# Output projection of a hybrid decoder block's second tokens in column passes, and its first expert block gathered in fp32

## The chip, the cores and the metric

The kernel runs on one core of one Trainium2 chip. The metric is device microseconds of one execution, the median of several. Every time below is in microseconds (us) unless marked ns.

## The reference

256 tokens of 1024 channels get 16 meta tokens ahead of them and pass one decoder layer: a state-space branch and a convolution branch, merged by gates, and then a mixture of 32 experts of which every token takes 4. What the change touches is the end of the first part and the experts:

```python
h = h + _hybrid_mixer(_rmsnorm(h, norm_mix_g), ...)      # ends in: merged @ w_out
h = h + _moe(_rmsnorm(h, norm_ffn_g), ...)
out = _rmsnorm(h, norm_final_g)[:, 16:]

def _rmsnorm(x, g):  return x * rsqrt(mean(x * x) + 1e-6) * g
def _moe(hf, ...):
    top_val, top_idx = lax.top_k(hf @ router_w + router_b, 4);  probs = softmax(top_val)
    for e in range(32):
        gu = hf @ w_gate_up[e] + b_gate_up[e];  g, lin = gu[:, :1024], gu[:, 1024:]
        g = min(g, 7);  lin = clip(lin, -7, 7)
        out += combine[:, e] * ((g * sigmoid(1.702 * g) * (lin + 1)) @ w_down[e] + b_down[e])
```

Everything is float32. The weights of one expert are 8.4 MB (gate and up) and 4.2 MB (down); all 32 experts' are read, 402.7 MB.

## The kernel before, in words

The tokens stand in two groups of 128, written c = 0 and c = 1. Each engine has its own program, and semaphores join them. `wait_ge` halts an engine's queue until a count is reached, and `link` makes an engine wait for its own last instruction.

**Up to the router.** TensorE (PE) computes the mixer in a fixed order. The output projection `merged @ w_out` is a loop over c, over eight slices k of 128 inputs and over two halves h of 512 outputs, in PSUM banks 4 + 2c + h (L1415 to 1433). Within c = 1, after k = 1, PE transposes the first tokens' residual (`residual_cols(0)`, L1401) and after k = 3 it multiplies them by the router (`logits(0)`, L1410); both follow for c = 1 after the loop. VectorE (DVE) has `second_norm(c)`: add the projection to the residual h2 (L1038), copy half of the transposed residual out of PSUM (L1041), the mean square (L1044), 1/sqrt by five linked operations (L761 to 765), and the normed tokens hf = h2 * scale * norm_ffn_g with the columns rearranged (L1050). ScalarE (ACT) copies the other half (L698), sums the squares (L701) and takes the root (L703). `choose(c)` (L1059 to 1074) is the top-4 choice: twelve small operations on 128x32 that end in `masks`. `weigh(c)` is the softmax of the four. DVE's order is second_norm(0), choose(0), weigh(0), second_norm(1), choose(1).

**Three bf16 parts.** A gather of tokens for an expert is a matmul with a one-hot matrix. So that it is exact in bf16, hf is split into three bf16 parts `hp`: ACT casts (L706, L709), GpSimd (POOL) subtracts (L572, L576), once for each c and half. `parts` counts what is done.

**Plan.** After both masks PE counts the tokens of each expert (L1542 to 1546), after it has put h2 into PSUM as the sum to which experts add (`residual`, L1442, eight matmul records ahead of the counting in PE's order). DVE makes positions and the first one-hot (L1104 to 1106, L1091), PE puts the bias (L1496) and gathers block 0 (L1450, 48 matmuls), ACT copies the gathered tokens to `xT` (L717), and PE begins with expert 0. The rest of the plan (which block is which expert, to `plan`) is computed between the first blocks' matmuls.

**Expert blocks.** A block is up to 64 tokens of one expert; here there are 35 blocks, so three experts have two. In `one_block` PE runs gate and up (L1476, eight slices k, of which two are one DMA piece of 2 MB), then `middle` (scatter of the block before, L1459; gather of the next, L1450; transposes, L1509 and L1514), then down (L1487, two DMA pieces of 2 MB). DVE clamps and multiplies, ACT has the sigmoid (L723) and the copies `actT` (L725), `xT` (L727) and `ysb` (L729).

**Weights.** SyncE (SP) issues the loads in a fixed order. Each waits until the buffer's last user on PE is done (`gu_done`, `dn_done`, L451 and L457); there are buffers for two experts, in `ring`, and the odd experts' first two pieces in `late` and `early`, over hf and h2. Expert 1's pieces 0 and 1 are issued after `parts` and after the counting matmuls.

**End.** After the last block ACT loads the Sqrt table (L739), squares both groups (L742) and DVE and ACT scale and store.

## Time and profile before

| what | value |
|---|---|
| runs | 1199.01 us median of 3 (1197.71 to 1199.34) |
| the profiled execution | 1199.63 us, its span from first to last instruction 1197.6 us |
| granted TensorE clock | 0.995 of full speed |
| busy share | PE 94%, DVE 27%, ACT 16%, POOL 4% |
| DMA | 436.43 MB, mean 364 GB/s, 428 to 430 GB/s in most slices of the second part |
| the first expert block begins | 237.05 us from the span's start |
| the last down projection begins | 1177.32 us |

The profiled execution's own time is 2.0 us over its span; the span is what views of the trace divide up. In a row of the timeline stand start, duration, engine, line of the kernel, operation, output <- inputs, shapes and count, and in brackets how long the engine had been idle and who released it. One float32 matmul with 128 columns of weights is two records, in `x16` too.

### The profile page before, as it was taken

The numbers are of one execution on the slowest core, as the hardware profiler recorded it, in microseconds if no ns is written. First come the engines' busy times: TensorE is split into PE (matmuls) and PEld (weight loads), VectorE is DVE, ScalarE is ACT, GpSimd is POOL, SyncE is SP. The second block draws the span as 40 slices with busy tenths as digits, with TensorE's granted clock in tenths as the row PEclk, the third lists the DMA queues.
The fourth block names the chain that finished last, engine by engine and source line by source line (L and its number), as shares of the span: only waits on it lengthen the run. The fifth ranks groups of instructions, "written<-read, shape, count | busy, mean of one in ns | idle before, by whom it ended". The sixth has DMA issues, their size and how long they took to land.

```text
span 1197.6 us, 17762 instructions
## 1 busy us (share of the span) xinstructions
PE 1127.9 (94%) x7148; PEld 532.1 (44%) x7149; DVE 324.9 (27%) x765; ACT 188.1 (16%) x279; POOL 43.8 (4%) x45
## 2 busy tenths in 40 slices
PE   8999999899999999989999998888888999999995
PEld 6887886443334333333343333333333334333332
DVE  5999462631122111111121111111111112111112
ACT  2311230411111111111111111111111111111002
POOL 1102230300000000000000000000000000000000
PEclk9999999999999999999999999999999999999998
DMA  9672593692999999997999999999999799999994
GB/s 263 216 203 94 202 386 123 242 408 100 430 429 428 429 428 428 429 428 310 414 429 428 428 428 429 429 428 429 429 429 428 334 387 429 429 427 428 428 428 177
DMA packets 57399, 436.43 MB, mean 364 GB/s; under 512 B 11056, under 2 KB 27504, under 8 KB 32704
## 3 DMA queue, kind: packets, MB, share of 16 engines
q1 hardware_dynamic: 57232, 436.02, 88.3%
q8 instruction: 16, 0.26, 0.1%
q10 hardware_dynamic: 144, 0.09, 0.0%
q14 instruction: 7, 0.06, 0.0%
HBM read 432.72 MB, written 1.05 MB: 362 GB/s over the span
## 4 chain that ended last, share of the span: by engine, by line
PE 70%; DMA 25%; ACT 2%; issue 1%; DVE 1%; ACTq 0%; SPq 0%; DVEq 0%
PE ps L1476 30%; DMA ring<-in_w_gate_up 25%; PE ps L1487 14%; PE ps L1238 8%; PE ps L1459 4%; PE ps L1450 2%; PE ps L1378 2%; PE ps L1425 2%; PE ps L1324 1%; PE ps L1509 1%; PE ps L1390 1%; ACT rD L725 1%; PE ps L1496 1%; PE ps L1289 0%; PE ps L1203 0%
## 5 line engine op out<-in xcount | busy, mean ns | idle before, releaser
L1476 PE MATMUL ps<-ring,rD 128*64 128x512 f32 x1664 | 368.1, 594 | 32.0 <-DMA ring<-in_w_gate_up 31.7
L1487 PE MATMUL ps<-ring,rD 128*64 128x512 f32 x1120 | 248.0, 595 | 16.0 <-ACT rD L725 15.9
L1476 PEld LDWEIGHTS ps<-ring,rD 128*64 128x64 f32 x1664 | 119.8, 137 | 266.0 <-issue 209.9
L1487 PEld LDWEIGHTS ps<-ring,rD 128*64 128x64 f32 x1120 | 79.8, 137 | 157.6 <-issue 157.3
L1160 DVE TENSOR_SCALAR rD<-ps 128x512 f32<-128x512 f32 x35 | 24.2, 691 | 424.3 <-PE ps L1476 424.3
L723 ACT ACTIVATE rD<-rD 128x512 f32<-128x512 f32 x35 | 22.0, 630 | 493.7 <-DVE rD L1160 493.7
L1238 PE MATMUL ps<-ring 128*128 128x256 f32 (+1 forms) x384 | 87.4, 386 | 0.0
L1086 DVE CAST rE<-rE 128x64 bf16 (+1 forms) x36 | 7.0, 195 | 294.4 <-PE ps L1476 294.1
L1238 PEld LDWEIGHTS ps<-ring 128*128 128x128 f32 x384 | 72.1, 190 | 12.7 <-issue 1.4
L1459 PE MATMUL ps<-rD,rE 64*128 64x512 f32 x288 | 71.6, 615 | 0.7 <-ACT rD L729 0.7
L1450 PEld LDWEIGHTS ps<-rE,rC 128*128 128x128 bf16 x1728 | 58.3, 99 | 27.3 <-issue 26.9
L1476 PE MATMUL ps<-late,rD 128*64 128x512 f32 x288 | 64.9, 592 | 0.0
L1476 PE MATMUL ps<-early,rD 128*64 128x512 f32 x288 | 64.9, 592 | 0.0
L1450 PE MATMUL ps<-rE,rC 128*128 128x64 bf16 x1728 | 63.5, 195 | 0.0
L729 ACT COPY rD<-ps 128x512 f32<-128x512 f32 x35 | 20.5, 585 | 243.7 <-PE ps L1487 243.7
L1459 PEld LDWEIGHTS ps<-rD,rE 64*128 64x128 f32 x288 | 24.8, 186 | 46.9 <-issue 45.4
L723 ACT ACT_TABLE_LOAD x32 | 41.1, 1283 | 6.3 <-DVEq L1123 5.7
L1476 PEld LDWEIGHTS ps<-early,rD 128*64 128x64 f32 x288 | 21.4, 137 | 40.4 <-issue 40.4
L1476 PEld LDWEIGHTS ps<-late,rD 128*64 128x64 f32 x288 | 21.2, 136 | 33.4 <-issue 30.4
L725 ACT COPY rD<-ps 128x512 f32<-128x512 f32 x35 | 20.5, 585 | 80.4 <-PE ps L1509 80.4
L1425 PE MATMUL ps<-ring,late 128*128 128x512 f32 x64 | 28.0, 593 | 0.0
L1378 PE MATMUL ps<-late,ring 128*128 128x256 f32 x128 | 27.8, 379 | 0.0
(332 smaller groups left out, 726.3 us busy)
## 6 DMA issues: line engine op xcount, KB each, us to landing
ring<-in_w_gate_up SPq DMA_DIRECT2D x96, 2048.0 KB, 20.6
ring<-in_w_down SPq DMA_DIRECT2D x64, 2048.0 KB, 24.5
late<-in_w_gate_up SPq DMA_DIRECT2D x16, 2048.0 KB, 24.4
early<-in_w_gate_up SPq DMA_DIRECT2D x16, 2048.0 KB, 28.8
ring<-in_w_in SPq DMA_DIRECT2D x14, 1024.0 KB, 7.9
ring<-in_w_out SPq DMA_DIRECT2D x4, 1024.0 KB, 17.0
ring<-late SPq DMA_DIRECT2D x16, 142.0 KB, 2.8
ring<-in_w_s_lin SPq DMA_DIRECT2D x2, 1024.0 KB, 5.0
```

Of the source, the lines that this page charges most:

```text
L723: nc.scalar.activation(sg, g1, ACT.Sigmoid, scale=ALPHA).then_inc(sg_ready, 1)
L725: nc.scalar.copy(actT, ps[:, 0, :].rearrange("p (j s) -> p j s", s=P)).then_inc(actT_ready, 1)
L729: nc.scalar.copy(ysb, ps[:, 2, :]).then_inc(y_ready, 1)
L1160: nc.vector.tensor_scalar(g1, ps[:, 0, :], LIMIT, None, ALU.min).then_inc(g1_ready, 1)
L1238: ins = nc.tensor.matmul(ps[:, z % 2, 0:L - n0], w[:, k, (z % 2) * P:(z % 2) * P + P], h[:, k, n0:L], start=(k == 0), stop=(k == KT - 1))
L1324: ins = nc.tensor.matmul(ps[32 * g:32 * g + 32, 3, (m % 2) * S:(m % 2) * S + S], wtap[:, a, g, :], shifted[:, m, g, SH * a:SH * a + S], st ...
L1378: ins = nc.tensor.matmul(ps[:, bank(use), g * S:(g + 1) * S], w[:, k, (n % 4) * P:(n % 4) * P + P], ya[:, k, :], start=(k == 0), stop=(k = ...
L1425: ins = nc.tensor.matmul(ps[:, 4 + 2 * c + h, :], merged[:, k, c * P:(c + 1) * P], w[:, k % 2, 512 * h:512 * h + 512], start=(k == 0), sto ...
L1450: ins = nc.tensor.matmul(ps[:, 3, k * BS:(k + 1) * BS], hp[:, part, c, k * P:(k + 1) * P], onehot[:, c, :], start=(c == 0 and part == 0), ...
L1459: ins = nc.tensor.matmul(ps[:, 4 + 2 * c + h, :], selT[64 * h:64 * h + 64, c * P:(c + 1) * P], ysb[64 * h:64 * h + 64, :], start=False, st ...
L1476: ins = nc.tensor.matmul(ps[64 * h:64 * h + 64, a, :], xT[:, k, :], gsl[odd][n][:, at:at + 512], start=False, stop=(k == KT - 1), skip_gro ...
L1487: ins = nc.tensor.matmul(ps[64 * h:64 * h + 64, 2, :], actT[:, k % 4, 64 * (k // 4):64 * (k // 4) + 64], dsl[odd][k // 4][:, at:at + 512], ...
```

## The change

1. The output projection of c = 1 is computed in three column passes (512, 256 and 256 outputs, each over all eight k) in banks 6, 7 and 4, and the transposes, the squares, the copies and the router matmuls of c = 1 are set between them, so that only those of the last 256 columns stand behind the last pass. c = 0's transposes come after k = 3 of the first pass, its router matmuls after k = 6.
2. hf is h2 times the row's scale, without norm_ffn_g, computed by ACT. The vector is put on the gathered tokens instead: DVE multiplies PSUM by `gains` into `xT`, for each block, where ACT copied. Its load is 4 KB in place of a 512 KB broadcast.
3. Block 0 is gathered in fp32 directly from h2 by 16 matmuls, with a one-hot `oh0` that holds the row scales. POOL's parts of c = 1 begin after that one-hot; the wait for `parts` stands in `middle`. Expert 1's piece 1 is issued after gather 0, piece 0 after `parts`.
4. `weigh(0)` and `weigh(1)` both come after the plan.
5. ACT calls Sigmoid on one element at the start of a block and Sqrt on one element after `actT`, so that the tables are there; the Sqrt call behind the blocks goes.
6. The last expert's last gate-up piece and its last down piece are each issued as two pieces of 1 MB, with the semaphores `gu_tail` and `dn_tail`, for which PE waits ahead of k = 7 and k = 6 in every expert.

```diff
+        WO_PARTS = [[(0, 512, 4), (512, 512, 5)], [(0, 512, 6), (512, 256, 7), (768, 256, 4)]]
+        TR_BANK = [[0, 1], [2, 3, 1]]
...
-            sp.dma_start(gffn, T["norm_ffn_g"][0:1, :].to_broadcast([P, D])).then_inc(late_in, 16)
+            sp.dma_start(gk, T["norm_ffn_g"].rearrange("o (p k) -> p (o k)", k=KT)).then_inc(late_in, 16)
...
-            sp.wait_ge(parts, 2 * ST)
-            first_gu(1, 0)
-            sp.wait_ge(count_mm, 1)
-            first_gu(1, 1)
+            sp.wait_ge(hf_ready, 2 * ST)
+            sp.wait_ge(gather_mm, 1)
+            first_gu(1, 1)
+            sp.wait_ge(parts, 2 * ST)
+            first_gu(1, 0)
...
+                rows = gu_rows(slice(e, e + 1), NPAIR - 1)
+                sp.dma_start(gsl[odd][NPAIR - 1][:, 0:SLOT], rows[:, 0:SLOT]).then_inc(gu_in[odd][NPAIR - 1], 16)
+                sp.dma_start(gsl[odd][NPAIR - 1][:, SLOT:], rows[:, SLOT:]).then_inc(gu_tail, 16)
...
             for c in range(ST):
+                if c == 1:
+                    pool.wait_ge(onehot_ready, 1)
...
+            def normalised(c):
+                act.wait_ge(row_scale, c + 1)
+                for a in range(2):
+                    ks = slice(4 * a, 4 * a + 4)
+                    nc.scalar.activation(hf[:, c, :].rearrange("t (k p) -> t k p", p=P)[:, ks, :],
+                                         by_k(h2[:, c, :])[:, ks, :], ACT.Copy, scale=ss[:, 12 + c:13 + c]
+                                         ).then_inc(hf_ready, 1)
...
             def one_block(i):
+                act.wait_ge(table, 2 * i + 1)
+                nc.scalar.activation(ss[:, 15:16], ss[:, 14:15], ACT.Sigmoid).then_inc(table, 1)
...
-                act.wait_ge(gather_mm, i + 2)
-                nc.scalar.copy(xT, ps[:, 3, :].rearrange("p (k s) -> p k s", s=BS)).then_inc(xT_ready, 1)
+                act.wait_ge(table, 2 * i + 2)
+                nc.scalar.activation(ss[:, 15:16], ss[:, 14:15], ACT.Sqrt).then_inc(table, 1)
...
-            link(nc.scalar.activation(ss[:, 15:16], ss[:, 14:15], ACT.Sqrt))
             for c in range(ST):
                 act.wait_ge(scattered, 2 * c + 2)
...
+            h2_part(0, 0)
+            h2_part(0, 1)
+            h2_cols(0, 1)
...
+            row_scales(0)
             choose(0)
-            weigh(0)
-            second_norm(1)
+            h2_part(1, 0)
+            h2_part(1, 1)
+            h2_cols(1, 1)
...
+            h2_part(1, 2)
+            h2_cols(1, 2)
...
+            row_scales(1)
             choose(1)
...
-            link(nc.vector.tensor_copy(cur[:, 0:2], posm[:, :, 0]))
-            onehot_for().then_inc(onehot_ready, 1)
+            for c in range(ST):
+                ins = nc.vector.tensor_scalar(oh0[:, c, :], slots[:, 0, :], posm[:, c, 0:1], ss[:, 12 + c:13 + c],
+                                              ALU.is_equal, ALU.mult)
+            ins.then_inc(onehot_ready, 1)
...
+            def gathered(n):
+
+                dve.wait_ge(gather_mm, n)
+                TT(xT, ps[:, 3, :].rearrange("p (k s) -> p k s", s=BS), gains, ALU.mult).then_inc(xT_ready, 1)
+
+            gathered(1)
...
+            for n, (at, width, b) in enumerate(WO_PARTS[1]):
                 for k in range(KT):
...
+                    if n == 2 and k == 0:
+                        pe.wait_ge(h2_ready, part_no(0, 0))
+                    ins = nc.tensor.matmul(ps[:, b, 0:width], merged[:, k, P:2 * P], wo[k // 2][:, k % 2, at:at + width],
+                                           start=(k == 0), stop=(k == KT - 1))
+                    if n == 0 and k == 3:
+                        residual_cols(0, 0)
+                        residual_cols(0, 1)
+                    if n == 0 and k == 6:
...
+                        logits(0, 0, KT)
+                    if n == 2 and k == 0:
+                        residual_cols(1, 0)
+                    if n == 2 and k in (1, 3, 5):
+                        ins.then_inc(wo_used, 1)
+                    if n == 2 and k == 3:
+                        residual_cols(1, 1)
+                    if n == 2 and k == 6:
+                        pe.wait_ge(h2T_act, 2)
+                        logits(1, 0, 4)
+                ins.then_inc(wo_mm, 1)
+            pe.wait_ge(h2T_dve, 2)
+            logits(1, 4, 6)
+            residual_cols(1, 2)
+            pe.wait_ge(h2T_dve, 3)
+            logits(1, 6, KT)
...
+                    elif n == NPAIR - 1:
+                        pe.wait_ge(gu_tail, e * 16 + 16)
...
                 pe.wait_ge(onehot_ready, i + 2)
+                pe.wait_ge(parts, 2 * ST)
                 gather(0, 6)
...
-            pe.wait_ge(parts, 2 * ST - 1)
-            gather(0, KT // 2)
-            pe.wait_ge(parts, 2 * ST)
-            gather(KT // 2, KT).then_inc(gather_mm, 1)
+            for k in range(KT):
+                for c in range(ST):
+                    ins = nc.tensor.matmul(ps[:, 3, k * BS:(k + 1) * BS], by_k(h2[:, c, :])[:, k, :], oh0[:, c, :],
+                                           start=(c == 0), stop=(c == 1))
+            ins.then_inc(gather_mm, 1)
```

`by_k` views h2's 1024 columns as 128 groups of 8, so slice k takes every eighth float32.

## Rows read from the trace of the kernel before

**Rows 1.** The page's section 4: shares of the chain that ended last, by engine.
```profile
PE 70%; DMA 25%; ACT 2%; issue 1%; DVE 1%; ACTq 0%; SPq 0%; DVEq 0%
```
**Rows 2.** That chain in order of time: start, us, what.
```profile
542.39 3.65 PE ps L1476 x16
...
1144.65 24.15 DMA ring<-in_w_gate_up
```
**Rows 3.** Windows: length, engines' busy us (records), granted clock, DMA share, GB/s.
```profile
272.00:295.00 23.00, 22.40 (x150) 9.06 (x148) 4.39 (x11) 3.65 (x5) 0.00 (x0) 1.00 0.07 27
561.00:571.00 10.00, 10.00 (x50) 3.52 (x48) 0.00 (x0) 0.00 (x0) 0.00 (x0) 1.00 0.17 52
```
**Rows 4.** Timeline of SP's queue: the first load behind the first gap.
```profile
295.10 0.33 SPq L451 DMA_DIRECT2D late<-in_w_gate_up  x1
```
**Rows 5.** Timeline of PE, from the projection of c = 1 to block 0.
```profile
207.68 1.04 PE L1401 MATMUL ps<-ident,early 128*128 128x128 f32 x8
208.56 3.60 PE L1425 MATMUL ps<-ring,late 128*128 128x512 f32 x8
211.99 1.87 PE L1410 MATMUL ps<-early,rD 128*128 128x32 f32 x16
...
220.80 1.44 PE L1401 MATMUL ps<-ident,early 128*128 128x128 f32 x8
...
224.92 3.68 PE L1442 MATMUL ps<-early,ident 128*128 128x512 f32 x8
...
233.64 2.74 PE L1450 MATMUL ps<-rE,rC 128*128 128x64 bf16 x48
```
**Rows 6.** Timeline of DVE, POOL and ACT in the same stretch.
```profile
217.03 1.08 DVE L1072 TENSOR_TENSOR rE<-rE 128x32 f32<-128x32 f32 x1
...
224.61 2.21 DVE L1050 SCALAR_TENSOR_TENSOR late<-early,ss 128x512 f32<-128x512 f32 x2
...
226.72 0.26 DVE L1059 SCALAR_TENSOR_TENSOR rE<-ps,ss,early 128x32 f32<-128x32 f32 x1
...
228.97 2.25 POOL L576 TENSOR_TENSOR rC<-late,rC 128x512 bf16<-128x512 f32 x2
...
230.20 1.07 DVE L1072 TENSOR_TENSOR rE<-rE 128x32 f32<-128x32 f32 x1
...
232.10 0.15 DVE L1104 COPY rE<-ps 32x1 f32<-32x1 f32 x1 [0.53 <-PE ps L1546]
...
236.41 0.58 ACT L717 COPY rD<-ps 128x512 f32<-128x512 f32 x1 [5.13 <-PE ps L1450]
```
**Rows 7.** DVE's groups by line and form: busy us, mean ns.
```profile
L1160 DVE TENSOR_SCALAR rD<-ps 128x512 f32<-128x512 f32 x35 | 24.2, 691 | 424.3 <-PE ps L1476 424.3
...
L949 DVE TENSOR_TENSOR_SCAN early<-sp_,early 128x136 f32<-128x136 f32 x32 | 11.1, 417 | 0.1
...
L1021 DVE TENSOR_TENSOR rE<-ps,rC 128x256 f32<-128x256 f32 x8 | 3.4, 424 | 6.3 <-PE ps L1390 6.3
...
L1067 DVE TENSOR_TENSOR_SCAN rE<-ones,rE 128x32 f32<-128x32 f32 x2 | 1.9, 961 | 0.0
...
L1079 DVE TENSOR_TENSOR rE<-rE 128x32 f32<-128x32 f32 x2 | 0.4, 192 | 0.1
```
**Rows 8.** Timeline of weight loads in a block: every fourth element, then packed.
```profile
1095.63 0.56 PEld L1509 LDWEIGHTS ps<-ident,rD 128*128 128x128 f32 x4
...
1096.10 0.26 PEld L1514 LDWEIGHTS ps<-ident,rE 128*128 128x128 f32 x2
```
**Rows 9.** Timeline of the end: PE's last two pieces, ACT behind the last block.
```profile
1163.95 3.65 PE L1476 MATMUL ps<-ring,rD 128*64 128x512 f32 x16 [0.39 <-DMA ring<-in_w_gate_up]
1168.85 3.65 PE L1476 MATMUL ps<-ring,rD 128*64 128x512 f32 x16 [1.24 <-DMA ring<-in_w_gate_up]
...
1186.58 1.28 ACT L739 ACT_TABLE_LOAD   x1 [1.54 <-issue]
...
1188.11 1.02 ACT L742 ACTIVATE rC<-ps 128x1024 f32<-128x1024 f32 x1
```

More of the change, by code:

```diff
@@ L451, in load_gu @@
                     sp.dma_start(gsl[odd][n], gu_rows(bass.ds(e, 1), n)).then_inc(gu_in[odd][n], 16)
+                if until == NPAIR:
+                    whole(gu_tail)
             def load_dn(e, odd, last):
@@ L457, in load_dn, with load_last @@
                     sp.dma_start(dsl[odd][h], dn_rows(bass.ds(e, 1), h)).then_inc(dn_in[odd][h], 16)
+                whole(dn_tail)
+            def load_last(last, before):
+                e, odd = EXP - 1, (EXP - 1) % 2
+                load_gu(e, odd, AHEAD, NPAIR - 1, last)
+                sp.wait_ge(gu_done, last * KT + KT)
+                rows = gu_rows(slice(e, e + 1), NPAIR - 1)
+                sp.dma_start(gsl[odd][NPAIR - 1][:, 0:SLOT], rows[:, 0:SLOT]).then_inc(gu_in[odd][NPAIR - 1], 16)
+                sp.dma_start(gsl[odd][NPAIR - 1][:, SLOT:], rows[:, SLOT:]).then_inc(gu_tail, 16)
+                sp.wait_ge(dn_done, before * KT + 4)
+                sp.dma_start(dsl[odd][0], dn_rows(slice(e, e + 1), 0)).then_inc(dn_in[odd][0], 16)
+                sp.wait_ge(dn_done, before * KT + KT)
+                rows = dn_rows(slice(e, e + 1), 1)
+                sp.dma_start(dsl[odd][1][:, 0:SLOT], rows[:, 0:SLOT]).then_inc(dn_in[odd][1], 16)
+                sp.dma_start(dsl[odd][1][:, SLOT:], rows[:, SLOT:]).then_inc(dn_tail, 16)
             for e in range(4):
@@ L478, in _ @@
             in_step(EXP - 7, 1)
-            for e in range(EXP - 6, EXP - 1):
+            for e in range(EXP - 6, EXP - 2):
                 last = used_by(e)
@@ L695, in _ @@
             link(nc.scalar.activation(ss[:, 15:16], ss[:, 14:15], ACT.Sqrt))
-            for c in range(ST):
-                act.wait_ge(h2_tr, 2 * c + 1)
-                nc.scalar.copy(h2T[:, 0:4, c * P:(c + 1) * P], ps[:, 2 * c, :].rearrange("p (k t) -> p k t", t=P)
-                               ).then_inc(h2T_act, 1)
-                act.wait_ge(h2_ready, 2 * c + 2)
-                nc.scalar.activation(squares, h2[:, c, :], ACT.Square, accum_out=ss[:, c:c + 1]).then_inc(sumsq, 1)
-                act.wait_ge(ms_ready, 2 + c)
-                nc.scalar.activation(ss[:, 9 + c:10 + c], ss[:, 6 + c:7 + c], ACT.Sqrt).then_inc(root, 1)
+            def normalised(c):
[5 more added lines that the diff above has]
+                                         ).then_inc(hf_ready, 1)
                 for a in range(2):
@@ L737, in _ @@
                             one_block(EXP + turn * TURNS + t)
-            link(nc.scalar.activation(ss[:, 15:16], ss[:, 14:15], ACT.Sqrt))
             for c in range(ST):
@@ L1126, in _ @@
             link(nc.vector.tensor_scalar(off, off, float(BS), None, ALU.mult))
-            weigh(1)
+            for c in range(ST):
+                weigh(c)
             nc.vector.engine_nop().then_inc(pos_ready, 1)
@@ L1405, in logits, with residual_cols @@
-            def logits(c):
-                pe.wait_ge(h2T_act, c + 1)
-                pe.wait_ge(h2T_dve, c + 1)
-                pe.wait_ge(rw_ready, 1)
-                for k in range(KT):
+            def residual_cols(c, n):
+                at, width, _ = WO_PARTS[c][n]
+                pe.wait_ge(h2_ready, part_no(c, n))
+                if c == 0 and n == 0:
+                    pe.wait_ge(merge_ready, 2 * KT)
+                for k in range(at // P, (at + width) // P):
+                    to = k * P - at
+                    ins = nc.tensor.transpose(ps[:, TR_BANK[c][n], to:to + P], h2[:, c, k * P:(k + 1) * P], ident[:, :])
+                ins.then_inc(h2_tr, 1)
@@ L1410, in logits @@
+            def logits(c, first, until):
+                for k in range(first, until):
                     ins = nc.tensor.matmul(ps[:, 2 * c, 0:EXP], h2T[:, k, c * P:(c + 1) * P], rw[:, k, :],
                                            start=(k == 0), stop=(k == KT - 1))
[L1412 to L1435 removed]
@@ L1436, in _ @@
-            residual_cols(1)
-            logits(1)
+                if until == KT:
+                    ins.then_inc(logit_mm, 1)
+            for k in range(KT):
+                if k == 0:
+                    emptied(pe, CO_USE + 5)
+                pe.wait_ge(merge_ready, KT + k + 1)
+                if k % 2 == 0:
+                    pe.wait_ge(wo_in[k // 2], 16)
+                for at, width, b in WO_PARTS[0]:
+                    ins = nc.tensor.matmul(ps[:, b, 0:width], merged[:, k, 0:P], wo[k // 2][:, k % 2, at:at + width],
+                                           start=(k == 0), stop=(k == KT - 1))
+                    if k == KT - 1:
+                        ins.then_inc(wo_mm, 1)
```

132 lines of the change are left out of this document (72 added, 60 removed).

## The prediction

> **What bounds the kernel now.** I read the chain that ended last first. By engine it is 70% PE and 25% DMA [rows 1], so neither engine's busy share says what a saved microsecond is worth. In order of time, PE carries it from the start to the first expert block and through the early blocks; then come stretches in which PE waits for w_gate_up pieces. One ends at 542.39, the last at 1144.65 + 24.15 = 1168.80 [rows 2].
>
> The windows say what ties these together. DMA runs at 428 to 430 GB/s through the expert part but for three gaps: in 272 to 295 its share is 0.07, in 561 to 571 it is 0.17 [rows 3], and a third like the second lies at 951 to 961. The gaps are the three experts with two blocks: their buffers stay in use for one PE block (26 us) more. What ends a gap is PE: SP issues the next piece at 295.10 [rows 4], when block 2, 58.05 us behind block 0's start at 237.05, has used its first piece. From there DMA is continuous to the next gap, which PE ends again. So if block 0 starts d earlier, the first gap ends d earlier, and so do the DMA stream, the later gaps and the end. A saving ahead of block 0 counts in full, one behind the last landing too; a saving per block counts only in blocks 0 to 2, in one block at each later gap and in the last half block.
>
> **Part 1 and 2: column passes.** Before, PE's work for c = 1 begins 4 matmuls ahead of the transposes at 207.68. 8 records of 512 columns take 3.60 [rows 5], 0.43 each without the drain, so it begins at 204.4. All of it to the projection's end is 32 records (13.7), 8 transposes (0.87) and 16 router records (1.71): 220.7, where the next transposes stand at 220.80 [rows 5]. After, the same 32 records' work comes with 6 transposes and 8 router records more ahead of its end: 0.65 + 0.86. That gives 222.2 without a stall.
>
> There is one stall. In PE's last pass, after its first k (at 217.7), the transposes of c = 1's first 512 outputs want the add h2_part(1, 0), and DVE's program has choose(0) ahead of it. That choice doesn't get shorter by starting earlier. Its two-input operations last until POOL's current subtraction ends: L1072 took 1.07 and ended at 231.27, POOL's L576 at 231.22, while a like operation takes 0.192 [rows 6, 7]. For c = 0 it is the same: L1072 ends at 218.11 [rows 6]. POOL's work for c = 0 keeps its place, as ACT's hf (two of some 0.6) takes the time of DVE's. So choose(0) ends near 218.5, the add (0.69 for 512 wide [rows 7]) near 219.3, and PE has stalled 1.6. The bounds are 0.6 (no pacing by POOL) and 2.2. I take 1.6, by the row of c = 0: the projection ends at 223.8, 3.0 later than before.
>
> Behind it less is left. Before, 3.81 us pass from 220.80 to the end of 1/sqrt at 224.61, then 2.21 of L1050, and choose(1) begins at 226.72 [rows 5, 6]. After, the adds and copies are 256 wide (0.42 [rows 7] for 0.69) and the squares a quarter of 1024 (1.02 for a like form [rows 9]; an estimate of 0.4). 3.81 - 0.27 - 0.6 gives 2.9; the copy of the first half no longer stands ahead of the squares, and I take 2.7. L1050 goes to ACT and off the path. choose(1) begins at 226.5. So columns and hf together give only 0.2.
>
> **choose(1) without POOL.** Before, from 226.72 to its last cast, 0.2 behind 231.27, it takes 4.8. POOL now waits for block 0's one-hot, so the stalls go: L1067, a scan of 32 columns, took 961 ns where scans of 136 columns take 417 [rows 7]; it should take some 0.25. With L1072 at 0.19, L1070 at 0.2 for 0.86 and one L1064 without 0.35 of stall the choice takes 2.35 and ends at 228.9.
>
> What is late next is PE. `residual` (8 records, 3.68 [rows 5]) stands ahead of the counting, behind the last router matmuls, which end near 225.5 after and at 224.9 before. It ends at 229.0 to 229.2. The counting follows at once and L1104 begins near 229.45, where it began at 232.10 [rows 6]: 2.65 gained. The bounds: nothing of the stalls goes, 0.3; a stall of 0.6 only, 3.6.
>
> **Part 3: block 0's gather.** From L1104 to the gather were 1.54 (232.10 to 233.64 [rows 5, 6]); a linked copy (0.19, [rows 7]) leaves the way and the one-hot is as wide as before: the gather starts at 230.8. It was 48 bf16 records in 2.74. Now it is 16 matmuls, 32 fp32 records, whose weight load bounds them: the router's 16 records took 1.87 [rows 5], 0.107 each without the drain. The weights are every eighth float32. The nearest row is L1509, whose weights are every fourth: its four loads take 1096.10 - 1095.63 = 0.47, 0.118 each [rows 8]. So 32 x 0.118 = 3.8, 1.05 more than before (bounds: 3.4, and 8.9 by the rival below). Then `gains` on DVE for ACT's copy: 0.69 [rows 7] for 0.58 [rows 6], 0.1 more. POOL's last subtraction of c = 1 ends about then, and if this operation waited for it as L1072 did it would cost up to 1.1; its first input is PSUM, and I take 0.
> The Trainium skill ("SBUF — State Buffer", section "Who interferes with whom") has VectorE wait for GpSimd where both its inputs are in SBUF, and not where one is; by that the 1.1 is no risk. The stalled L1072 reads two in SBUF and so agrees; no row here shows an operation with PSUM beside a subtraction of POOL.
>
> Block 0 starts at 230.8 + 3.8 + 0.7 = 235.3: **1.75 earlier**.
>
> **What hides the rest.** The parts of c = 1 are ready near 235, `middle` asks for them near 250. weigh(0) and weigh(1) add 0.9 to the plan between PE's pieces; the transposes that want them have 0.4 to spare against the first two pieces of 3.65, so a few tenths could show. Expert 1's pieces are issued near 234.5 and 235 for 231.25 and 232; with the pieces behind them they land by 264, and block 1 wants the third at 271: 7 us of cover. dn(1, 0) goes from 212 to 221 (`wo_used` counts in the last pass), wanted at 282. The 4 KB vector saves 0.5 MB (1.2 us of DMA) where PE doesn't wait for DMA: 0. In the blocks the new waits of PE are for counts long reached, and its records stand back to back: 0. `gains` in a block stands beside down (7.1 us): 0. ACT's two table loads (1.28 each) stand beside down and gate-up: 0; if the order were such that Sigmoid's came after g1, it would cost 1.28 in some 5 blocks.
>
> **Parts 5 and 6: the end.** Before, the third piece of expert 31 starts at 1163.95 and ends at 1167.6, PE idles 1.24, and the fourth starts at 1168.85 [rows 9]. After, its first half has landed by then (it is 1 MB, 2.4 us, ahead of the second), k = 6 runs from 1167.6 to 1169.4 and k = 7 follows; the half that lands at 1168.85 is there. Gained: the idle time, **1.24**, not the 1.8 of a half piece. The halves of down don't matter: its pieces land by 1178, and it wanted the second at 1180.8. Behind the last block ACT's table load starts at 1186.58 and the squares at 1188.11 [rows 9]. The load goes, the issue time of 1.54 ahead of it stays, and scatter of c = 0 is done by then: **1.45**. DVE and the root behind it hang on these squares.
>
> **Sum.** 1.75 + 1.24 + 1.45 = 4.4. The profiled execution (1199.63, span 1197.6) becomes 1195.2, span 1193.2. It stood 0.6 over the median; the median goes from 1199.0 to **1194.6**.
>
> **The rivals.**
> 1. Strided weights (slower). Each of the 32 weight loads reads every eighth float32, 32 bytes apart, and the price is that of the row which reads so: L1050, 2.21 for two of 512 elements, 2.16 ns an element [rows 6]. A load of 128 is then 0.277, the gather 8.9 and not 3.8: +5.1, median 1199.7. It outweighs the rest from (3.8 + 4.4) / 32 = 0.256 us a load on. Against it: L1509 at 16 bytes pays nothing, and L1050 read two such inputs. The Trainium skill has the rule for it ("SBUF — State Buffer", section "Door 1: The DMA port swizzle"): an access that leaves a 16-byte line pays, so fp32 may step by four at most for free. By its letter the change's gather pays and L1509 hardly; how much, it doesn't say.
> 2. The stall behind choose(0) doesn't occur. If POOL's work moves against DVE's, PE's last pass runs through: 1.6 more, 1193.0. But PE's `residual` is as near, so I expect half of it at most.
> 3. The table comes back. If Sqrt is loaded again ahead of the last root, 1.0 of the 1.45 is lost: 1195.6.
> 4. Longer gaps in the blocks. Before down PE waits now 0.33, now 0.6 us behind `actT`, by turns; if the changed program makes all of them long, 0.27 in some 4.5 blocks on the path: 1195.8.
> 5. The start is paced elsewhere (gains held by POOL for 1.1, the plan's transposes late, weights at 0.16 a load): the 1.75 shrinks to nothing, only the end's 2.7 is left: 1196.3.
>
> **How the numbers follow.** The forecast gets 0.54, the rivals in turn 0.07, 0.12, 0.08, 0.10, 0.09. About 0.2% (2.4 us) is what can be told from no change, so "faster" is below 1196.6: 0.50 of the forecast, and 0.12, 0.07, 0.07 and 0.04 of rivals 2 to 5 give 0.80; I take 0.79. Slower by as much needs rival 1 with more behind it: 0.04. The rest, 0.17, is within. The bounds of the stall (-1.0, +0.6), of the choice (+2.3) and of the gather (-0.4, up to +1.4 at half of rival 1's extra) around 1194.6 give 1192.2 to 1197.9; with rival 2 in and rival 1 out I take 1192.0 to 1197.9.
>
> **What would show it.** Block 0's first L1476 at 235.3 in the trace after (237.05 before); the projection's end at 223.8, with DVE's add of c = 1's first part behind choose(0); no operation of choose(1) over 0.3; the fp32 gather 3.8 long; the first load behind the first gap at 293.35; no idle time ahead of expert 31's fourth piece; no table load behind the last block. It is wrong if the three terms are there and the time is not (then a gap of DMA doesn't hang on PE), or if the gather takes over 6 us.

## The result: slower by 0.2%

| | median | lowest to highest | runs |
|---|---|---|---|
| before | 1199.78 us | 1197.71 to 1202.08 | 20 |
| changed | 1202.16 us | 1200.31 to 1204.91 | 20 |

The ratio is 1.002, 95% interval 1.0014 to 1.0027: 2.4 us slower, where 4.4 faster was forecast. The profiled execution of the changed kernel took 1200.99, its span 1198.9 at a granted clock of 0.993; it lies 1.2 under the median of its 20, so the trace below accounts for 1.3 of the 2.4 us.

In the timeline of PE in the changed kernel (columns as in [rows 5]) the projection ends a little before 223.3, and the gather is the first thing that is badly off:

```profile
218.44 0.66 PE L1491 MATMUL ps<-ident,early 128*128 128x128 f32 x4 [0.87 <-DVE early L1103]
...
222.55 0.68 PE L1517 MATMUL ps<-ring,late 128*128 128x256 f32 x2
...
225.24 3.68 PE L1546 MATMUL ps<-early,ident 128*128 128x512 f32 x8
...
230.67 7.89 PE L1662 MATMUL ps<-rE,early 128*128 128x64 f32 x32
...
239.34 5.52 PE L1582 MATMUL ps<-ring,rD 128*64 128x512 f32 x16 [0.47 <-DVE rD L1197]
```

It took 7.89 for 2.74 before [rows 5], where 3.8 was forecast. The second surprise is the last row: the first 16 records of block 0 take 5.52, where the same form takes 3.65 elsewhere [rows 9].

The timeline of DVE beside it shows that the choice did what was expected. The stretched operations of choose(0) come ahead of the add that PE waits for; those of choose(1) are gone:

```profile
216.50 1.07 DVE L1135 CAST rE<-rE 128x32 bf16<-128x32 f32 x1
...
217.69 1.02 DVE L1103 TENSOR_TENSOR early<-early,ps 128x512 f32<-128x512 f32 x2
...
226.08 0.25 DVE L1121 SCALAR_TENSOR_TENSOR rE<-ps,ss,early 128x32 f32<-128x32 f32 x1
...
227.08 0.21 DVE L1129 TENSOR_TENSOR_SCAN rE<-ones,rE 128x32 f32<-128x32 f32 x1
...
228.12 0.17 DVE L1136 TENSOR_SCALAR rE<-rE 128x32 f32<-128x32 f32 x1
229.22 0.15 DVE L1180 COPY rE<-ps 32x1 f32<-32x1 f32 x1 [0.92 <-PE ps L1655]
...
238.60 0.69 DVE L1197 TENSOR_TENSOR rD<-ps,colp 128x512 f32<-128x512 f32 x1 [6.17 <-PE ps L1662]
```

The windows of PE's clock say where the 5.52 comes from. Columns: window, length, then busy us (records) of PE, PEld, DVE, ACT, POOL, the granted clock, the DMA share and GB/s. First the kernel before, from ahead of its gather to the first two pieces of block 0:

```profile
224.00:233.60 9.60, 5.47 (x27) 2.74 (x26) 8.40 (x25) 4.08 (x6) 4.74 (x4) 1.00 0.53 200
233.70:237.00 3.30, 3.00 (x54) 2.72 (x52) 0.23 (x2) 0.58 (x1) 0.00 (x0) 0.50 0.95 407
237.05:244.00 6.95, 6.95 (x34) 2.63 (x36) 2.47 (x14) 1.28 (x1) 0.00 (x0) 1.00 0.94 370
```

Then the changed kernel:

```profile
224.00:232.90 8.90, 7.38 (x33) 4.60 (x32) 6.42 (x27) 6.75 (x12) 2.75 (x3) 1.00 0.95 394
232.90:243.10 10.20, 9.73 (x38) 6.92 (x39) 1.37 (x6) 0.17 (x1) 1.76 (x2) 0.50 0.35 129
243.20:250.00 6.80, 6.80 (x36) 2.39 (x34) 3.15 (x15) 1.68 (x3) 0.00 (x0) 1.00 1.00 424
```

Clock 0.50 is the lower level, 1.2 GHz, 1.00 is 2.4. Before, in this trace, the low stretch lay on the bf16 gather and was over at block 0. After, it begins in the gather and reaches 3.8 us into block 0.

SP's queue carries the difference on. The load that ends the first gap stood at 295.10 [rows 4]:

```profile
299.16 0.33 SPq L472 DMA_DIRECT2D late<-in_w_gate_up  x1
```

It is 4.06 later: 2.29 by which block 0 starts later (239.34 for 237.05), 1.87 of the clock on its first slices, -0.10 elsewhere. The loads behind the second and third gap are 4.3 and 4.2 later. The windows of the gaps still show DMA nearly idle while PE works (columns as above, compare [rows 3]):

```profile
277.00:299.00 22.00, 21.40 (x146) 8.72 (x144) 4.91 (x12) 4.77 (x7) 0.00 (x0) 1.00 0.12 49
565.00:575.00 10.00, 10.00 (x48) 3.42 (x46) 0.00 (x0) 0.00 (x0) 0.00 (x0) 1.00 0.13 33
```

At the end some 3 us come back. Timeline of PE, then ACT, in the last block, against [rows 9]:

```profile
1168.16 7.09 PE L1582 MATMUL ps<-ring,rD 128*64 128x512 f32 x32 [0.49 <-DMA ring<-in_w_gate_up]
...
1180.07 7.09 PE L1595 MATMUL ps<-ring,rD 128*64 128x512 f32 x32 [0.59 <-ACT rD L791]
...
1189.33 1.02 ACT L807 ACTIVATE rC<-ps 128x1024 f32<-128x1024 f32 x1 [1.54 <-PE ps L1563]
```

The last down projection starts 2.75 later than before (1177.32), not 4.18: the pieces in halves gave 1.43. The squares are 1.22 later (1188.11 before): the table gave 1.53. The span is 1.3 longer.

### The profile page after: what moved, and what is told of

The parts are those of the page before. It is cut to its first block, busy times and chain, and to the rows that moved or that the text cites. A ratio compares the mean times of both kernels' runs of the same rounds, so it can differ in the third digit from the quotient of the medians.

```text
span 1198.9 us, 18007 instructions
## 1 busy us (share of the span) xinstructions
PE 1134.0 (95%) x7148; PEld 540.5 (45%) x7149; DVE 340.7 (28%) x801; ACT 231.3 (19%) x355; POOL 43.4 (4%) x45
## 4 chain that ended last, share of the span: by engine, by line
PE 71%; DMA 25%; ACT 1%; issue 1%; DVE 1%; ACTq 0%; SPq 0%; DVEq 0%
PE ps L1582 30%; DMA ring<-in_w_gate_up 25%; PE ps L1595 14%; PE ps L1327 8%; PE ps L1563 4%; PE ps L1467 2%; PE ps L1554 2%; PE ps L1413 1%; PE ps L1479 1%; PE ps L1618 1%; PE ps L1509 1%; ACT rD L791 1%; PE ps L1604 1%; PE ps L1517 1%; PE ps L1662 1%
## 5 line engine op out<-in xcount | busy, mean ns | idle before, releaser
L1554 PEld LDWEIGHTS ps<-rE,rC 128*128 128x128 bf16 x1680 | 55.7, 98 | 26.9 <-issue 26.5
L1554 PE MATMUL ps<-rE,rC 128*128 128x64 bf16 x1680 | 60.8, 193 | 0.0
```

The lines of the kernel that those rows point to most:

```text
L1554: ins = nc.tensor.matmul(ps[:, 3, k * BS:(k + 1) * BS], hp[:, part, c, k * P:(k + 1) * P], onehot[:, c, :], start=(c == 0 and part == 0), ...
```

## The experiments

The theory after the result: each of the gather's 32 weight loads pays for its step of eight floats (+4.1 us), and the granted clock, which falls in this gather, adds some 1.9 on block 0; the rest of the change works. The rivals: the loads are long because the clock is low; or fp32 in itself is what costs; or the parts that were forecast to gain don't. The experiments come in the order in which they ran; each is an edit of the changed kernel, but for before_end, which is one of the kernel before, and packed_hf_weigh, one of packed_hf. Each is compared with executions of the kernel before that ran beside it.

**packed_weights.** The weights are 128 neighbours. The blocks are then fed wrong channels (xT is not the reference's).

```diff
-    matmul(ps[:, 3, k * BS:(k + 1) * BS], by_k(h2[:, c, :])[:, k, :], oh0[:, c, :], ...
+    matmul(ps[:, 3, k * BS:(k + 1) * BS], h2[:, c, k * P:(k + 1) * P], oh0[:, c, :], ...
```

> The changed kernel, but block 0's fp32 gather takes 128 adjacent float32 of h2 as its weights where it took every eighth (this leaves out the rearrangement of block 0's channels; nothing else of the work differs). Stride theory: a weight load of 128 columns that lie 32 bytes apart takes 0.2375 us whatever the clock is, packed ones 0.107; the gather's 32 records take 3.5 us and not 7.8, block 0 begins at 234.9 for 239.3, and the time is 4.4 us under the changed kernel's 1202.2, 1197.8; if the granted clock is back at full when block 0 begins, its first two slices take 3.65 for 5.52 and the time is 1195.9. Clock theory (the gather is long because the clock was at half in 6 of its 8 us): the gather stays above 6 us and the time within 1 us of 1202.2.

Measured: 1196.22 (8 runs), before 1200.07 (19 runs), ratio 0.9967, 0.9955 to 0.9979. PE's timeline:

```profile
226.67 5.38 PE L1546 MATMUL ps<-early,ident 128*128 128x512 f32 x8
...
233.81 3.79 PE L1662 MATMUL ps<-rE,early 128*128 128x64 f32 x32
...
238.37 3.65 PE L1582 MATMUL ps<-ring,rD 128*64 128x512 f32 x16 [0.56 <-DVE rD L1197]
```

The loads are 0.1115 apart for 0.2375, the gather is 3.8 long, which is the forecast's figure for it, and block 0 runs at full clock. The low stretch came earlier in this execution, from 226.9 to 230.3, and made `residual` 1.7 longer. So 5.9 us (1202.16 to 1196.22) go with one address pattern, 4.1 of them in the gather itself, and the same program comes out on the other side of the kernel before. fp32 in itself is not the cause: packed, it costs what was forecast.

**stride_ladder.** Slice k of the gather reads its weights with a step of k + 1 elements. The channels are again the wrong ones.

```diff
-    by_k(h2[:, c, :])[:, k, :]
+    h2[:, c, 0:P * (k + 1)].rearrange("t (p j) -> t j p", j=k + 1)[:, 0, :]
```

> The changed kernel, but slice k of block 0's gather reads its weights with a step of k + 1 float32, so steps 1 to 8 stand side by side, four records each (block 0's channels are then not the right ones). Line theory: the steps 1 to 4 (up to 16 bytes) take 0.107 to 0.12 us a record, 5 to 8 take 0.2375 each, together 16 x 0.11 + 16 x 0.2375 = 5.6 us. If the price grows evenly with the step, the records go from 0.107 to 0.2375 in steps of 0.019 and the sum is 5.5 us as well, so the spacing of single records decides. Clock theory: the spacing follows the granted clock and not the step.

Measured once: 1201.24, the gather 6.46 long. The distance between the starts of successive weight loads and the recorded length of one, by step (the median of four loads each):

```
step (fp32)      1      2      3      4      5      6      7      8
apart, us     0.110  0.118  0.173  0.233  0.221  0.223  0.231  0.237
length, us    0.190  0.197  0.261  0.330  0.315  0.317  0.327  0.335
```

Windows of the same gather (columns as above, PEld second):

```profile
231.29:233.00 1.71, 1.71 (x15) 1.71 (x13) 1.68 (x2) 1.25 (x4) 1.71 (x3) 1.00 1.03 441
233.00:234.50 1.50, 1.50 (x8) 1.50 (x8) 0.04 (x1) 0.62 (x1) 1.50 (x3) 0.90 0.06 22
234.50:236.00 1.50, 1.50 (x9) 1.50 (x8) 0.00 (x0) 0.00 (x0) 0.76 (x1) 0.50 0.00 0
```

The clock halves at 234.2, and the loads go on as before: eight or nine records start in 1.5 us on either side. So the clock doesn't make the loads long; the step does. A step of two is free or nearly so, and from four on the whole price is paid. Neither expected course came: the steps of 3 and 4 aren't free, and the price doesn't grow evenly. The Trainium skill ("SBUF — State Buffer", section "Door 1: The DMA port swizzle") has two sentences on this: full bandwidth needs at least two hits in a 16-byte line, and fp32 may therefore step by 4 for free. This ladder bears out the first (a step of 2 still has two floats in a line, a step of 3 not always, from 4 on there is one) and not the second: a step of 4 costs as much as one of 8. (Both hold for the loads of matmuls; those of transposes, below, behave otherwise.)

**bf16_gather.** Part 3 undone: the first block is gathered from the bf16 parts again, `parts` is waited for ahead of it, and POOL doesn't wait for the one-hot. The rest of the change stays.

```diff
...
-                if c == 1:
-                    pool.wait_ge(onehot_ready, 1)
...
-            for k in range(KT):
-                for c in range(ST):
-                    ins = nc.tensor.matmul(ps[:, 3, ...], by_k(h2[:, c, :])[:, k, :], oh0[:, c, :], ...)
+            pe.wait_ge(parts, 2 * ST)
+            gather(0, KT).then_inc(gather_mm, 1)
```

> The changed kernel with part 3 undone: block 0 is gathered in 48 bf16 matmuls from the three parts again, POOL doesn't wait for the one-hot, ScalarE makes the second parts ahead of the exponentials. Stride theory: the gather takes 2.7 us; choose(1) is held by POOL again (4.8 us from 226.1, to 230.9, for 231.5 in the kernel before), so block 0 begins near 236.5, 0.5 us ahead of the kernel before, and with 2.7 to 3.0 us saved at the end the time is 3.3 us under the kernel before, 1196.5. If instead something else of the change costs (the waits for the tails, the multiplication by the norm vector), block 0 begins at 236.5 and the time is still above 1199.

Measured: 1196.3 (6 runs), before 1200.07, ratio 0.9967, 0.9955 to 0.9979. The timelines of PE and of ACT:

```profile
232.73 0.62 PE L1599 MATMUL ps<-rW,rE 96*64 96x512 bf16 x4 [3.41 <-DVE rE L1151]
233.79 2.74 PE L1549 MATMUL ps<-rE,rC 128*128 128x64 bf16 x48 [0.44 <-POOL rC L615]
...
237.32 3.65 PE L1577 MATMUL ps<-ring,rD 128*64 128x512 f32 x16 [0.46 <-DVE rD L1192]
```
```profile
226.33 2.33 ACT L740 ACTIVATE late<-early,ss 128x512 f32<-128x512 f32 x2 [1.06 <-DVEq L1114]
```

Here the gather waits for POOL, and POOL's work hangs on ACT, which needs 2.33 for hf with its rearranged columns. Block 0 starts at 237.32, and not near 236.5 as expected: no earlier than before (237.05), so columns and hf on ACT give nothing by themselves, where the prediction had 0.2. What this trace gains, it gains at the end: the last down projection starts 0.62 earlier than before, the squares 2.15. Its execution (1197.48) is 1.2 over the median of the six; some 0.9 of the medians' 3.8 stand in no trace. To free the start from the parts, as part 3 does, is right, as packed_hf shows below; the way it reads is not.

**before_end.** The kernel before with parts 5 and 6 alone.

```diff
+                act.wait_ge(table, 2 * i + 1)
+                nc.scalar.activation(ss[:, 15:16], ss[:, 14:15], ACT.Sigmoid).then_inc(table, 1)
...
-            link(nc.scalar.activation(ss[:, 15:16], ss[:, 14:15], ACT.Sqrt))
...
+                sp.dma_start(gsl[odd][NPAIR - 1][:, 0:SLOT], rows[:, 0:SLOT]).then_inc(gu_in[odd][NPAIR - 1], 16)
+                sp.dma_start(gsl[odd][NPAIR - 1][:, SLOT:], rows[:, SLOT:]).then_inc(gu_tail, 16)
```

> The kernel before with parts 5 and 6 of the change alone (the tables called early, the last pieces in halves). If the end's terms stand by themselves: 1.24 to 1.4 us from the halves and 1.45 from the table, 2.8 us under the kernel before, 1197.0, with block 0 at 237.05 as before. If the waits added in every block or the two table loads per block cost anything, the blocks (26.07 and 25.81 us) get longer and the gain is below 2 us.

Measured: 1197.78 (12 runs), before 1200.07, ratio 0.9977, 0.9967 to 0.9988: 2.3 us faster. The forecast had 2.7 for these parts; the traces of before and after give 1.43 + 1.53 = 2.96.

This trace shows something else besides. Up to block 0 PE's work is that of the kernel before, with the bf16 gather, and yet the clock is low far into block 0, whose first 16 records take 6.23 (PE's timeline, then windows, columns as above):

```profile
236.59 6.23 PE L1509 MATMUL ps<-ring,rD 128*64 128x512 f32 x16 [0.36 <-ACT rD L743]
```
```profile
228.20:231.50 3.30, 1.53 (x8) 0.45 (x6) 2.63 (x8) 2.14 (x3) 2.11 (x2) 1.00 0.24 50
231.60:241.70 10.10, 9.17 (x68) 4.47 (x70) 1.60 (x11) 0.59 (x1) 0.00 (x0) 0.50 0.92 389
```

So the long low stretch isn't the strided gather's alone. The mean granted clock of each execution tells how often there may be one: it was 0.992 or 0.993 in all 20 of the changed kernel, while of the 19 of the kernel before 13 had 0.995 or 0.996 (median 1199.8), five 0.992 (1201.5) and one 0.994. This execution had 0.992 as well. (That the low stretch stood in about the same place in all of them is an inference; only the profiled executions show where it was.)

**packed_hf.** A version that could beat both: the fp32 gather reads hf, whose columns ACT has already put in order, so its weights are packed. The one-hot holds no scales then, and POOL's subtractions, which overwrite hf, begin after the gather.

```diff
-                    by_k(h2[:, c, :])[:, k, :], oh0[:, c, :], ...
+                    hf[:, c, k * P:(k + 1) * P], oh0[:, c, :], ...
...
-            second_parts(0)                      # ACT, between hf(0) and hf(1)
+            second_parts(0)                      # ACT, behind weigh's exponentials
...
+            pool.wait_ge(gather_mm, 1)           # POOL, ahead of all its parts
-                if c == 1:
-                    pool.wait_ge(onehot_ready, 1)
```

> The changed kernel with block 0 gathered in fp32 from hf, which ScalarE has written with each slice's 128 channels side by side, and a plain fp32 one-hot; POOL's subtractions begin only after this gather (they change hf in place), and ScalarE's second parts of both groups come last. Stride theory: the gather takes 3.6 us; choose(0) is no longer held by POOL (2.1 us for 4.9), so PE's stalls in the last passes (1.2 us) go too, and block 0 begins 5.5 us ahead of the changed kernel, near 233.8, 3.2 ahead of the kernel before. With 2.8 us at the end the time is 6.0 under the kernel before: 1194.0, and 1195 if the granted clock is at half in some of that stretch. Rival: the parts come too late now (POOL done near 242), pieces of expert 1 with them, and the gain is lost by block 1: not under 1196.5.

Measured: 1195.23 (6 runs), before 1199.78 (17 runs), ratio 0.9963, 0.9949 to 0.9977. PE, then two rows of DVE's timeline:

```profile
230.22 3.79 PE L1662 MATMUL ps<-rE,late 128*128 128x64 f32 x32
...
234.79 3.65 PE L1581 MATMUL ps<-ring,rD 128*64 128x512 f32 x16 [0.56 <-DVE rD L1196]
...
244.14 0.61 PE L1680 MATMUL ps<-ident,rE 128*32 128x128 f32 x4 [1.54 <-DVEq L1215]
```
```profile
235.45 0.95 DVE L1204 TENSOR_SCALAR rE<-rE 32x48 f32<-32x48 f32 x1
...
240.91 1.09 DVE L1140 TENSOR_TENSOR rE<-rE 128x32 f32<-128x32 f32 x1
```

Block 0 starts 2.3 earlier than before, though 1.0 later than the 233.8 expected (the time is 1.2 over the expected one), and the granted clock is 1.00 until the last matmul is done. But POOL subtracts until 243, DVE's small operations beside it are stretched again (1.09 for the 0.19 of L1140), now in the plan, and PE stands idle for 1.54 us ahead of the plan's transposes in block 0.

**dense_gather.** The changed kernel with its strided gather, and 16 bf16 matmuls of 512 columns, whose result nobody reads, one between each two slices.

```diff
+                    nc.tensor.matmul(ps[:, 2, :], onesb[0:96, :], bp[:, 0:512], start=True, stop=True)
```

> The changed kernel with its strided fp32 gather, and behind each of its 16 matmuls one bf16 matmul of 512 columns into a bank that nobody reads (extra work, result unchanged). It keeps TensorE's array streaming while the strided weights are loaded. If the granted clock falls in the changed kernel because the array gets few columns during the gather, it stays at full here, the first two slices of expert 0 take 3.65 us and not 5.5, and the time is 1.0 to 1.5 us under the changed kernel's 1202.2 although the gather is up to 0.9 longer. If the clock falls for what happened ahead of the gather, nothing changes but the 0.9: 1203. In both the 32 strided loads stay at 0.2375 us apart or more, as the stride theory has it.

Measured: 1200.76 (12 runs), before 1199.78, ratio 1.0016, 1.0005 to 1.0028. The windows of the gather and of block 0's first slices:

```profile
231.30:240.70 9.40, 9.06 (x54) 8.65 (x52) 2.48 (x4) 1.89 (x5) 3.99 (x4) 1.00 0.21 87
240.70:245.00 4.30, 4.30 (x22) 1.72 (x24) 0.66 (x5) 0.00 (x0) 0.00 (x0) 1.00 0.99 366
```

With the added matmuls the granted clock stays at 1.00 in this trace. Block 0 begins at 240.70, 1.36 later than in the changed kernel, 0.72 by the added work and 0.64 because the gather itself began later (at 231.31), and yet the first load behind the gap comes at 298.72, 0.44 earlier. From block 0's start to that load are 58.02 us, as before the change (58.05), for 59.82 with the low clock: 1.8 us are the clock's. The median moved with it, to 1.0 over the kernel before, for 2.4, as expected. But the added matmuls don't always help: nine of the 12 executions had a mean clock of 0.996 to 0.998 and took 1200.1 to 1201.1, three had 0.991 and took 1204.0 to 1204.6. No trace was taken of those three.

**packed_hf_weigh.** packed_hf with weigh(0) and weigh(1) ahead of gathered(1) in DVE's order, where DVE is idle.

> As packed_hf, with the two weigh(c) calls (the gating weights that the down projections use) put ahead of gathered(1) in VectorE's order, where VectorE is idle between 231 and 234 us. Theory (the plan's operations, held up by GpSimd's subtractions, make PE's third piece wait until 244.14): with weigh done early the plan's positions are ready at about 241, the third piece starts about 1.5 us earlier at 242.6, and the restart of the stream comes at about 292.8 instead of 294.35; time about 1193.7 against packed_hf's 1195.2. Rival: the remaining operations of the plan are stretched by the same GpSimd subtractions wherever they stand, or the DMA of the third piece sets the start; then nothing is gained, restart 294.3 and 1195.2.

Measured: 1193.63 (1193.32 to 1194.03, 5 runs), before 1199.64 (9 runs), ratio 0.9947, 0.9934 to 0.9961: 6.0 us under the kernel before, the best of all. The third piece follows without a gap:

```profile
238.12 3.65 PE L1581 MATMUL ps<-ring,rD 128*64 128x512 f32 x16
241.71 0.61 PE L1680 MATMUL ps<-ident,rE 128*32 128x128 f32 x4
242.25 3.65 PE L1581 MATMUL ps<-ring,rD 128*64 128x512 f32 x16
```

The load behind the first gap, with which the DMA stream restarts, comes at 291.92, 57.95 behind block 0's start, for 59.56 in packed_hf: 1.6, where the theory gave 1.5, and the medians differ by 1.6 too. (In this execution block 0 also began 0.8 earlier than in packed_hf's, ahead of anything the edit touches.)

**changed_again, changed_again2.** The changed kernel, unaltered, for two more traces.

> The changed kernel once more, unaltered, for a second trace. In the first trace the granted clock fell to half at 232.9 us, inside the gather, for 10.24 us, and block 0's first slices took 5.5 us per pair for 3.65. Theory (the strided weight loads cost 4.1 us whatever the clock does; the clock's fall adds about 1.9 where it lies on block 0): the gather again starts at 230.7 and takes 7.8; the low stretch may lie elsewhere or last 3.4 or 10.2 us, and the restart (299.16 in the first) moves by up to 2 us with it, to 297.2 or to 301. Rival: the low clock always falls in the same place, and the restart is at 299.2 to within 0.3 us.

> The changed kernel a third time, unaltered, for a third trace. As for changed_again: the gather starts at 230.7 and takes 7.8 us whatever the clock does (theory), and the place and length of the low stretch differ between the traces, with the restart following it; by the rival all three traces show the same stretch and the same restart.

Measured: 1202.19 and 1201.75. The windows of changed_again:

```profile
224.20:227.50 3.30, 3.30 (x8) 1.75 (x8) 2.77 (x17) 2.25 (x3) 0.00 (x0) 0.50 1.04 407
227.70:234.30 6.60, 5.59 (x26) 3.78 (x24) 3.11 (x8) 4.04 (x7) 3.26 (x3) 1.00 0.61 258
234.40:244.60 10.20, 9.74 (x37) 6.36 (x39) 1.37 (x6) 0.00 (x0) 1.15 (x2) 0.50 0.42 154
```

The gather took 7.88 in both. The low stretch moves: it begins at 232.9, 234.4 and 234.4, so it covers 3.8, 4.4 and 5.1 us of block 0, and from block 0's start to the restart are 59.82, 60.14 and 60.54. changed_again has a second one on `residual` besides, which starts its gather at 231.56 for 230.67. That is a reason for the first trace's +1.3 where the medians have +2.4: its low stretch cost least of the three. Three traces don't settle what it costs on average, but no execution of the changed kernel had a mean clock over 0.993.

**transpose_ladder.** One row was still against all this: L1509, whose fp32 weights have a step of 4 and whose loads start 0.118 apart [rows 8], where the ladder has 0.233. So the changed kernel got two ladders more ahead of its gather, 16 transposes and 16 matmuls with the same weights and 128 columns of the identity, two for each step; nobody reads them.

```diff
+            for j in range(KT):
+                for c in range(ST):
+                    src = h2[:, c, 0:P * (j + 1)].rearrange("t (p j) -> t j p", j=j + 1)[:, 0, :]
+                    nc.tensor.transpose(ps[:, 2, 0:P], src, ident[:, :])
+            for j in range(KT):
+                for c in range(ST):
+                    src = ...
+                    nc.tensor.matmul(ps[:, 2, 0:P], src, ident[:, :], start=True, stop=True)
```

> The changed kernel with 32 more instructions ahead of block 0's gather, whose results nobody reads: 16 fp32 transposes of h2 and then 16 fp32 matmuls with the same weights against the identity (two records each), both with weight steps of 1 to 8 elements, two instructions for each step. Question: why were the loads of the blocks' transposes (L1509, step 4) only 0.12 us apart, where the ladder of matmuls has 0.233 at step 4? Theory (in a transpose the matmul of 128 columns sets the distance and hides the load, whose own length grew): the transposes are 0.11 to 0.12 apart up to step 4, their loads' lengths grow from 0.14, and the 128-column matmuls, covered by the same stream, are nearer together than the 64-column ones of the ladder (0.233 at step 4). Rival: a load for a transpose is cheaper in itself; then the transposes stay at 0.11 to 0.12 up to step 8, while the matmuls of 128 columns repeat the ladder of those of 64: 0.11, 0.118, 0.173, 0.233, 0.22, 0.22, 0.23, 0.237. Time some 7 us over the changed kernel's 1202: 1209.

Measured once: 1211.29, beside a before of 1201.57. In PE's timeline the 16 records of the transposes are L1663, the 32 of the matmuls L1667, and the gather is L1670:

```profile
233.20 2.12 PE L1663 MATMUL ps<-ident,early 128*128 128x128 f32 x16
235.16 6.37 PE L1667 MATMUL ps<-ident,early 128*128 128x128 f32 x32
241.37 7.78 PE L1670 MATMUL ps<-rE,early 128*128 128x64 f32 x32
```

The loads of the two new groups, by step (the mean of two for the transposes, the median of four for the matmuls; the very first distance, 0.057, is left out):

```
step (fp32)              1      2      3      4      5      6      7      8
transposes: apart    0.111   0.113  0.116  0.118  0.118  0.126  0.129  0.118
  length, us         0.140   0.199  0.199  0.208  0.206  0.230  0.222  0.202
matmuls: apart       0.112   0.118  0.173  0.233  0.227  0.224  0.230  0.237
  length, us         0.192   0.197  0.261  0.330  0.321  0.318  0.326  0.335
```

My theory falls: 128 columns in place of 64 hide nothing, the matmuls repeat the first ladder to within 6 ns. They ran wholly at a clock of 1.00 (it fell at 242.9), the first ladder's steps of 5 to 8 at 0.50 but for the first two loads, so this is a second sign that the clock isn't it. The rival holds. Of one stored operand and one step, a transpose's loads start some 0.12 apart and a matmul's up to 0.237. The transposes' loads do feel a step in their length (0.14 packed, 0.20 to 0.23 from 2 on), but not in their distance. Why, no run here tells.

## Why the prediction was wrong

- **The step that failed** is the gather's term: "its four loads take 1096.10 - 1095.63 = 0.47, 0.118 each [rows 8]. So 32 x 0.118 = 3.8". It was 32 x 0.2375 = 7.6, and 7.9 with the end of the last matmul: 4.1 us more, enough to take back all but 0.3 of the 4.4. The prediction's own sign of being wrong, "if the gather takes over 6 us", came. Rival 1, "Strided weights (slower)", had the mechanism, a price a little too high (0.277 a load for 0.2375) and a chance far too low (0.07), because of "L1509 at 16 bytes pays nothing". By its own threshold of 0.256 a load the stride alone would not have outweighed the rest; that the kernel became slower took the clock besides.
- **Why the row misled.** L1509's loads belong to transposes. transpose_ladder shows that those hardly feel a step (0.118 apart at 4 and at 8), while an fp32 matmul with the very same weights pays the whole (0.233 and 0.237). The number 0.118 was right, and right for another form of instruction. The row had a hint of it: its loads are 0.212 long, those of the packed L1514 0.146. But by length alone the price would have come out at 32 x 0.07 = 2.1, half of what it was.
- **The clock wasn't in the sum at all.** It costs 1.8 to 1.9 on block 0 in the first trace, 2.1 and 2.5 in the other two. Without it the change would stand at -4.4 + 4.1, within what can be told from nothing; the clock makes it slower. dense_gather's trace keeps the clock and shows its price, but not that time, as its added matmuls cost 0.7 themselves. The kernel before can lose time in the same way (before_end), but did so in fewer executions. What makes the clock fall stays open. On record is how often the mean clock of an execution was 0.993 or less: all 20 of the changed kernel, 5 of 12 of before_end, 5 of the 19 of the kernel before, 3 of 12 of dense_gather, 1 of 8 of packed_weights, none of the 6 of bf16_gather and none of the 11 of the two packed_hf kernels.
- **The projection** ended at 223.2 (forecast 223.8): the stall behind choose(0) was there, paced by POOL (L1135 1.07), but only 0.87 of it stood as idle PE, for 1.6. Rival 2 (no stall) didn't come, and the 0.6 by which the projection was early brought nearly nothing, since `residual` ended where it was forecast.
- **choose(1)** began at 226.1 for 226.5 and took 2.2 for 2.35 (the savings that the prediction lists, 0.88, 0.66, 0.71 and 0.35 of 4.8, give 2.2 themselves); no operation over 0.25, the scan 0.21 for 0.25. `residual` ended at 228.9 for 229.0 and L1180 (L1104 before) came at 229.22 for 229.45: 2.9 gained for 2.65. The gather began at 230.67 for 230.8. `gains` took 0.69 and was not held by POOL, neither here, where POOL had ended at 234.7, nor in packed_hf, where it began just ahead of POOL. "No row here shows an operation with PSUM beside a subtraction of POOL" overlooks L1059 [rows 6], which reads PSUM and took 0.26 at 226.72, with POOL's L572 running from 226.48 to 229.00. After the change L1103 with 512 columns, one input in PSUM, took 0.69 beside POOL's L617.
- **How a start is carried on** held: 4.06 later at the first gap, 4.3 and 4.2 at the others, none of it lost in the DMA-bound stretches. So the wrong term weighed in full.
- **The range** took in +1.4 for the gather, "at half of rival 1's extra"; half of that 5.1 is 2.6. The step that failed is thus in the range too, at a bound too low.
- **The end**: halves 1.43 for 1.24, table 1.53 for 1.45. Rivals 3 and 4 didn't come: L793's table load lies beneath the down projection, and PE's idle time behind `actT` is 16.1 us in 35 blocks both before and after.
- Put the other way: with packed weights and nothing else altered (packed_weights) the difference to before is -3.9, where the forecast was -4.4.

Open stays whether ACT's strided read in hf (L742, 2.34 for two, forecast as some 0.6 each) could be had for less, why the clock falls and in which executions, and how much of the medians' 2.4 is its.

## What to carry to other kernels

An fp32 matmul of few columns is as fast as its weight load (here with 64 and 128 columns), and from a step of four elements on such loads start twice as far apart as packed ones: rearrange the operand where another engine writes it anyway (here ACT, in hf), not in the weights' address pattern. A price taken from a trace holds for the form of instruction that the row shows; when the row nearest in step is of another form (a transpose for a matmul), keep the mechanism's full price in the range and a chance on it that matters. Look at the mean granted clock of every execution and not of the profiled one alone, since the clock takes more than one course in the same kernel. And where work moves out of the way, look for who then stands beside it: POOL's subtractions held up the choice before, and the plan after.

## What the runs showed of the hardware

- fp32 weight loads of 128 columns, for matmuls: 0.110 us apart packed, 0.118 at a step of 2, 0.173 at 3, 0.22 to 0.24 from 4 to 8 (stride_ladder, transpose_ladder). From 5 to 8 they are the same within 6 ns at a granted clock of 1.00 and of 0.50; the lower steps ran at 1.00 only.
- Loads for fp32 transposes: 0.11 to 0.13 apart for every step from 1 to 8 (transpose_ladder).
- The granted clock fell from 1.00 to 0.50 in the strided gather in each of the changed kernel's three traces (at 232.9, 234.4, 234.4) and stayed low for some 10.2 us, far into block 0. It did the same with the bf16 gather in before_end's trace (231.6 to 241.8), and fell for 3.4 us in those of before, bf16_gather and packed_weights. In the traces of packed_hf, packed_hf_weigh and dense_gather it didn't fall up to the end of the matmuls, though the mean clock of three other executions of dense_gather was 0.991.
- While POOL subtracts (2.27 for two of 512), DVE's small operations may take up to 1.1 for 0.19, and the stretched ones end within 0.1 us of the end of one of POOL's (packed_hf: L1140 at 242.00, POOL's L616 at 241.94). Moving POOL's work moves the stall to whichever of DVE's operations then stand beside it.
